# Moving the start addresses of the rounded weight halves in a two-block transformer kernel

## The chip, the cores and the metric

The kernel runs on one core of one Trainium2 chip. The metric is the device time of one execution in microseconds (us), from the first to the last instruction and what lies around it. Three runs of the kernel before gave 2228.66 us as the median, 2226.96 us the lowest and 2229.32 us the highest.

## The reference

Two transformer blocks run one after the other on 256 tokens of width 1024, all in float32, each with two layers. The first block has a modulated norm, a gated delta rule with 8 heads, a sliding-window attention with 16 heads, three projections and a gated feed-forward part with a short convolution. The second has a mixer (sparse attention chosen by an indexer, and a chunked mLSTM) between two feed-forward parts. Nearly all arithmetic is in products of the activations with large weight matrices:

```
for l in range(DEPTH):                       # first block
    proj = h @ w_in[l]                       # 1024 x 7440
    y_a = o_dn @ w_dn_out[l]; y_b = attention @ w_swa_out[l]
    x = x + gt1 * (merged @ w_o[l])
    up_act, up_lin = jnp.split(h @ w_up[l], 2, axis=-1)
    x = x + gt2 * ((jax.nn.silu(up_act) * up_lin) @ w_down[l])
for l in range(DEPTH):                       # second block
    x = x + 0.5 * swiglu(rmsnorm(x, ffn1_norm[l]), ffn1_w_gate[l], ffn1_w_up[l], ffn1_w_down[l])
    x = x + hybrid_mixer(...)                # h @ w_in, and @ w_out at its end
    x = x + 0.5 * swiglu(rmsnorm(x, ffn2_norm[l]), ffn2_w_gate[l], ffn2_w_up[l], ffn2_w_down[l])
```

## The kernel before

The weights stream through SBUF in chunks of 1 MB: eight blocks of 128 rows by 256 columns, or, for the products back from the hidden width, two blocks of 128 rows by 1024 columns. SP issues one DMA for a chunk into one of three ring slots (`ring`). To keep float32 precision with the faster rounded type of TensorE, a chunk is split into two halves. ScalarE copies it with rounding into the high half (`weights_high`, the `split` of the scalar block, line 2178); VectorE subtracts the high half from the ring slot and so makes the low half (`weights_low`, `split` of the vector block, line 1441). The activations are kept as a high and a low half too (`h_high`, `h_low`, and `hidden_high`, `hidden_low` in the feed-forward parts).

TensorE then makes three products for each tile of 128x128 weights: high weights by high activations, high weights by low activations, and low weights by high activations. In `linear3` these are lines 753, 754 and 755, in `linear3_tiles` 731 to 733 and in `down_tile` 991 to 993. Each of the three loads 128x128 weights as the stationary operand and streams 256 columns of activations, so a chunk is 48 pairs of a weight load and a matmul. `token_major3` (lines 784 to 786) has the roles exchanged: the activations are stationary and 256 columns of a weight half stream past.

Of the 314 chunks 304 are split. They are numbered n = 0 to 303 in the order of the schedule (`SPLIT`, `SI`). The halves of chunk n lie in pair n % 2 of two pairs of stores, so that one pair is written while the other is read. ScalarE waits, before it writes the high half of chunk n, until TensorE is done with chunk n - 2 (`chunk_multiplied`); VectorE waits for ScalarE (`chunk_rounded`), TensorE for VectorE (`chunk_split`). Two of the 304 chunks are wide ones with 272 columns a block (the first chunk of a layer of the first block, `s1`); the other 302 are called narrow here.

The four stores follow one another in the arena, 8768 bytes apart. In the built program they begin at bytes 127360, 136128, 144896 and 153664 of a partition. `shifts` lets each half begin 12 elements (48 bytes) into its store. The activation tiles (`h_high` at byte 52608, `h_low` at 60800, `hidden_high` at 70016) begin at 128 modulo 256. A row of a stationary tile is 512 bytes in a partition, and the tiles of a chunk lie multiples of 512 bytes apart, so that all tiles of one half have the same start modulo 256:

| half | store | start, bytes modulo 256 |
|---|---|---|
| high, even n | 0 | 176 |
| low, even n | 1 | 240 |
| high, odd n | 2 | 48 |
| low, odd n | 3 | 112 |

Of the kernel before, what the change touches and what calls it, by code (L numbers as in the profile page):

```python
# [20 lines left out]
T = 256  # L21
D = 1024
KT = D // P
# [8 lines left out]
WIDE = 272  # L32
# [142 lines left out]
def build(nc, a, out):  # L175
# [24 lines left out]
    with ExitStack() as ctx:  # L200
# [26 lines left out]
        def rounded(name, at, *shape):  # L227

            return nc.alloc_sbuf_tensor_at(name, [P] + list(shape), F32R, offset=arena_at + 4 * at)
# [12 lines left out]
        def ar(at, *shape):  # L242
            n = int(np.prod(shape))
            v = arena[:, at:at + n]
            if len(shape) == 2:
                return v.rearrange("p (a b) -> p a b", a=shape[0])
            if len(shape) == 3:
                return v.rearrange("p (a b c) -> p a b c", a=shape[0], b=shape[1])
            return v
# [18 lines left out]
        oH, oL = rounded("out_high", 8192, KT, T), rounded("out_low", 10240, KT, T)  # L268
        half_names = ("weights_high0", "weights_low0", "weights_high1", "weights_low1")
        half_stores = [rounded(n, 14336 + (SLOT + 16) * i, SLOT + 16) for i, n in enumerate(half_names)]  # L270
        shifts = (12, 12, 12, 12)
        half = lambda i, n: half_stores[i][:, shifts[i]:shifts[i] + KT * n].rearrange("p (t n) -> p t n", t=KT)
        WH, WL = ([half(2 * i + low, T) for i in range(2)] for low in range(2))
        wide_high, wide_low = ([half(2 * i + low, WIDE) for i in range(2)] for low in range(2))
        hW = ar(12288, KT, T)
        ktok = [ar(11264, 2, 2, P), ar(9216, 2, 2, P)]
        XV = ar(11264, 2, 512)
# [245 lines left out]
        def release(key):  # L523

            kind, l, i = key
            if kind == "turn":
                return rope_added, 5 * l + ROPE.index(i) + 1
            if kind == "adr":
                return mod_ready, GROUPS.index((l, i)) + 1
            if kind == "qkv":  # L530
                return conv_done, 12 * l + i + 1
            if kind == "qk":
                return (conv_scaled, 2 * l + i + 1) if i < 2 else (conv_done, 24 + 4 * l + i + 1)
            if kind in ("aq", "qi"):
                return q_scaled, 3 * l + 2 * (kind == "qi") + i + 1
            if kind in ("swq", "z", "ga", "gb", "vm", "om"):
                return in_copied, INC[key]
            if kind in ("dno", "swo"):
                return merged, 8 * l + 4 * (kind == "swo") + i + 1
            if kind == "wo":  # L540
                return x_done, X0["wo", l] + 2 * i + 2
            if kind == "out":
                return x_done, X0["out", l] + i + 1
            if kind == "ua":
                return fconv_done, FP * l + i + 1
            fi = {"ul": l, "g1": 2 + 2 * l, "u1": 2 + 2 * l, "g2": 3 + 2 * l, "u2": 3 + 2 * l}[kind]
            if kind[0] == "g":
                return gate_scaled, FP * (fi - 2) + i + 1
            return hidden_ready, FP * fi + i + 1
# [7 lines left out]
        for key in R:  # L557
            at = key[2] % 3 if key[0] == "qkv" else R[key] % 2
# [52 lines left out]
        def halves(n):  # L611

            if SPLIT[n][0] == "s1":
                return wide_high[n % 2][:, :, :], wide_low[n % 2][:, :, :]
            return WH[n % 2][:, :, :], WL[n % 2][:, :, :]

        landed = {}
        total = [0] * NS
# [94 lines left out]
        def _(pe):  # L713
# [3 lines left out]
            def linear3_tiles(key, high, low, order, pairs, made):  # L717

                n = SI[key]
                wh, wl = WH[n % 2], WL[n % 2]  # L720
                pe.wait_ge(chunk_split, n + 1)
                pe.wait_ge(*release(PREV[key]))
                o = PLACE[key]
                for m in range(2):
                    for t in order:
                        if pairs is not None and m == 0 and t < 4:
                            pe.wait_ge(pair_copied, pairs + t + 1)
                        if pairs is not None and m == 0 and t == 4:
                            pe.wait_ge(*made)
                        a_, b_ = wh[:, t, m * P:(m + 1) * P], wl[:, t, m * P:(m + 1) * P]  # L730
                        mm(o[:, m, :], a_, high[t], start=(t == order[0]), stop=False)
                        mm(o[:, m, :], a_, low[t], start=False, stop=False)
                        last = mm(o[:, m, :], b_, high[t], start=False, stop=(t == order[-1]))
                last.then_inc(chunk_multiplied, 1)

            def linear3(key, high, low, norm=None, ready=None, between=None):

                n = SI[key]
                wh, wl = WH[n % 2], WL[n % 2]
                pe.wait_ge(chunk_split, n + 1)  # L740
                if PREV[key] is not None:
                    pe.wait_ge(*release(PREV[key]))
                o = PLACE[key]
                for m in range(2):
                    for t in range(KT):
                        if (m, t) == (1, KT // 2) and between is not None:
                            between()
                        if norm is not None and m == 0:
                            pe.wait_ge(norm_ready, KT * norm + t + 1)
                        if ready is not None and m == 0 and t % 2 == 0:  # L750
                            pe.wait_ge(ready[0], ready[1] + t // 2 + 1)
                        a_, b_ = wh[:, t, m * P:(m + 1) * P], wl[:, t, m * P:(m + 1) * P]
                        mm(o[:, m, :], a_, high[:, t, :], start=(t == 0), stop=False)  # L753
                        mm(o[:, m, :], a_, low[:, t, :], start=False, stop=False)  # L754
                        last = mm(o[:, m, :], b_, high[:, t, :], start=False, stop=(t == KT - 1))  # L755
                last.then_inc(chunk_multiplied, 1)
# [15 lines left out]
            def token_major3(key, dst, norm=None):  # L772

                n = SI[key]
                wh, wl = halves(n)
                pe.wait_ge(chunk_split, n + 1)
                if key in R:
                    pe.wait_ge(*release(PREV[key]))
                for tt in range(2):
                    for t in range(KT):  # L780
                        if norm is not None and tt == 0:
                            pe.wait_ge(norm_ready, KT * norm + t + 1)
                        a_, b_ = h_high[:, t, tt * P:(tt + 1) * P], h_low[:, t, tt * P:(tt + 1) * P]
                        mm(dst(tt), a_, wh[:, t, :], start=(t == 0), stop=False)
                        mm(dst(tt), a_, wl[:, t, :], start=False, stop=False)
                        last = mm(dst(tt), b_, wh[:, t, :], start=False, stop=(t == KT - 1))
                last.then_inc(chunk_multiplied, 1)
# [191 lines left out]
            def down_start(kc, l, i, fi):  # L979

                n = SI[kc, l, i]
                pe.wait_ge(chunk_split, n + 1)
                pe.wait_ge(hidden_ready, FP * fi + i + 1)
                return (w[n % 2][:, :, :].rearrange("p a b -> p (a b)") for w in (WH, WL))

            def down_tile(wh, wl, i, t, m):

# [76 lines left out]
            def head_tiles(*tiles):  # L1064

                n = SI["s1", 0, 0]
                wh, wl = halves(n)
                pe.wait_ge(chunk_split, n + 1)
                for t in tiles:
                    pe.wait_ge(norm_ready, t + 1)  # L1070
                    for tt in range(2):
                        a_, b_ = h_high[:, t, tt * P:(tt + 1) * P], h_low[:, t, tt * P:(tt + 1) * P]
                        to = B[4 + tt][:, 0:WIDE]
                        mm(to, a_, wh[:, t, :], start=(t == 0), stop=False)
                        mm(to, a_, wl[:, t, :], start=False, stop=False)
                        last = mm(to, b_, wh[:, t, :], start=False, stop=(t == KT - 1))
                if tiles[-1] == KT - 1:
                    last.then_inc(chunk_multiplied, 1)
# [24 lines left out]
            for v in range(1, 8):  # L1103
                n = V_ROWS[v % 3] if v < 6 else V_ROWS[3]
# [204 lines left out]
            for l in range(LAYERS):  # L1309
# [79 lines left out]
                for c in range(2):  # L1389
                    for j in range(4):  # L1390
                        n = 4 * c + j
# [18 lines left out]
                for i in range(4):  # L1410
                    linear3_tiles(("out", l, i), merged_high, merged_low, range(KT), pairs if i == 0 else None, (m_split, l + 1))
# [1328 lines left out]
```

## Time and profile before

| | |
|---|---|
| median of three runs | 2228.66 us |
| the profiled execution | 2228.63 us |
| its span, first to last instruction | 2226.8 us |
| mean granted TensorE clock | 0.992 of full speed |
| TensorE matmuls (PE) busy | 2145.2 us, 96% of the span |
| TensorE weight loads (PEld) busy | 2043.7 us, 92% |
| VectorE (DVE) | 1505.3 us, 68% |
| ScalarE (ACT) | 1077.0 us, 48% |
| GpSimd (POOL) | 580.9 us, 26% |
| moved by DMA | 383.93 MB, 172 GB/s on average |

Matmuls are pipelined: the profile gives each a duration of some 280 ns, and the next one begins long before that has passed. How fast TensorE works is read from the distance of the starts. PE are the matmuls, PEld the weight loads; a wait is put down to the instruction that ended last before it was over.

### The profile page before, as it was taken

What the parts mean: (1) busy time and instruction counts of PE and PEld (TensorE: products, weight loads), DVE (VectorE), ACT (ScalarE), POOL (GpSimd) and SP (SyncE); (2) the same over time, 40 slices, a digit from 0 to 9 for tenths busy, and PEclk for the clock granted to TensorE, in tenths of its full rate; (3) what the DMA queues carried; (4) which work ended last, traced back from release to release, by engine and by line L of the source; (5) the groups of instructions that cost most, each with busy time, mean ns of one, the idle gap of its engine ahead of it and who ended that gap; (6) DMA issues with size and microseconds to landing.
All of it is one profiled execution on the core that took longest, in us unless ns stands there. A gap on an engine that the chain in (4) does not pass through costs nothing.

```text
span 2226.8 us, 39796 instructions
## 1 busy us (share of the span) xinstructions
PE 2145.2 (96%) x17221; PEld 2043.7 (92%) x17221; DVE 1505.3 (68%) x1850; ACT 1077.0 (48%) x1432; POOL 580.9 (26%) x280
## 2 busy tenths in 40 slices
PE   7999999999999999999999999989999999999999
PEld 4988899899998888989999999879999999879999
DVE  6967775787678766667666556876556556786555
ACT  3666573433356647443445435554445444555333
POOL 0963324899248260475000000100000000100000
PEclk9999999999999999999999999999999999999999
DMA  9752336677656315566555555335555555434553
GB/s 320 236 170 81 108 121 198 225 252 239 205 181 216 96 41 168 171 213 205 188 184 176 186 184 166 110 96 189 189 188 172 189 184 177 133 95 149 182 185 129
DMA packets 332856, 383.93 MB, mean 172 GB/s; under 512 B 12551, under 2 KB 315402, under 8 KB 332554
## 3 DMA queue, kind: packets, MB, share of 16 engines
q1 hardware_dynamic: 332234, 381.23, 53.6%
q8 instruction: 136, 2.23, 0.4%
q14 instruction: 38, 0.31, 0.0%
q10 hardware_dynamic: 448, 0.16, 0.0%
HBM read 380.32 MB, written 1.05 MB: 171 GB/s over the span
## 4 chain that ended last, share of the span: by engine, by line
PE 75%; DVE 15%; ACT 7%; issue 3%; DMA 0%; SPq 0%; ACTq 0%; DVEq 0%
PE bank L753 16%; PE bank L754 15%; PE bank L755 15%; DVE weights_low L1441 6%; PE bank L993 5%; PE bank L992 5%; PE bank L991 5%; ACT weights_high L2178 4%; DVE arena L1569 2%; PE bank L769 1%; PE bank L892 1%; PE bank L1210 1%; PE bank L1225 1%; PE bank L884 1%; PE bank L1047 1%
## 5 line engine op out<-in xcount | busy, mean ns | idle before, releaser
L1441 DVE TENSOR_TENSOR weights_low<-ring,weights_high 128x2048 fp32r<-128x2048 f32 (+1 forms) x304 | 759.2, 2497 | 431.6 <-ACT weights_high L2178 431.0
L753 PE MATMUL bank<-h_high,weights_high 128*128 128x256 f32 x3296 | 937.9, 285 | 23.7 <-DVE weights_low L1441 14.3
L755 PE MATMUL bank<-h_high,weights_low 128*128 128x256 f32 x3296 | 925.8, 281 | 0.0
L754 PE MATMUL bank<-h_low,weights_high 128*128 128x256 f32 x3296 | 923.0, 280 | 0.0
L2178 ACT ACTIVATE weights_high<-ring 128x2048 fp32r<-128x2048 f32 (+1 forms) x304 | 582.2, 1915 | 693.3 <-PE bank L755 537.1
L753 PEld LDWEIGHTS bank<-h_high,weights_high 128*128 128x128 f32 x3296 | 622.0, 189 | 43.4 <-DVE weights_low L1441 23.8
L754 PEld LDWEIGHTS bank<-h_low,weights_high 128*128 128x128 f32 x3296 | 620.6, 188 | 3.4 <-issue 3.3
L755 PEld LDWEIGHTS bank<-h_high,weights_low 128*128 128x128 f32 x3296 | 620.3, 188 | 0.0
L991 PE MATMUL bank<-hidden_high,weights_high 128*128 128x256 f32 x1056 | 295.3, 280 | 1.4 <-DVE hidden_low L1707 0.9
L993 PE MATMUL bank<-hidden_high,weights_low 128*128 128x256 f32 x1056 | 296.2, 281 | 0.0
L992 PE MATMUL bank<-hidden_low,weights_high 128*128 128x256 f32 x1056 | 295.2, 280 | 0.0
L2657 POOL TENSOR_TENSOR side<-side,ccol 128x1024 f32<-128x1024 f32 x80 | 206.2, 2598 | 305.4 <-DVE out_low L1674 133.0
L2635 POOL TENSOR_TENSOR side<-swq 128x512 f32<-128x512 f32 x4 | 8.2, 2076 | 814.0 <-DVE swq L2022 814.0
L991 PEld LDWEIGHTS bank<-hidden_high,weights_high 128*128 128x128 f32 x1056 | 199.1, 189 | 2.0 <-issue 1.1
L992 PEld LDWEIGHTS bank<-hidden_low,weights_high 128*128 128x128 f32 x1056 | 198.3, 188 | 0.0
L993 PEld LDWEIGHTS bank<-hidden_high,weights_low 128*128 128x128 f32 x1056 | 198.3, 188 | 0.0
L2658 POOL TENSOR_TENSOR side<-side 128x1024 f32<-128x1024 f32 x40 | 127.3, 3181 | 3.1
L1569 DVE SCALAR_TENSOR_TENSOR arena<-bank,vcol,arena 128x254 f32<-128x254 f32 (+2 forms) x256 | 111.3, 476 | 3.7
L2659 POOL TENSOR_TENSOR side<-side 128x512 f32<-128x512 f32 x40 | 85.1, 2129 | 3.1
L2329 ACT ACTIVATE hidden_high<-arena 128x512 fp32r<-128x512 f32 x66 | 41.0, 621 | 72.0 <-DVE arena L1704 72.0
L1717 DVE TENSOR_TENSOR arena<-bank,rinv 128x512 f32<-128x512 f32 x44 | 30.4, 692 | 56.3 <-PE bank L755 50.5
L1704 DVE TENSOR_TENSOR arena<-arena,bank 128x512 f32<-128x512 f32 x66 | 45.1, 684 | 33.6 <-DVE arena L1720 27.7
(439 smaller groups left out, 2817.7 us busy)
## 6 DMA issues: line engine op xcount, KB each, us to landing
ring<-in_w_in SPq DMA_DIRECT2D x80, 1024.0 KB, 5.3
ring<-in_w_up SPq DMA_DIRECT2D x44, 1024.0 KB, 5.3
ring<-in_ffn_w_gate SPq DMA_DIRECT2D x44, 1024.0 KB, 5.4
ring<-in_ffn_w_up SPq DMA_DIRECT2D x44, 1024.0 KB, 5.4
ring<-in_ffn_w_down SPq DMA_DIRECT2D x44, 1024.0 KB, 5.0
side<-in_w_ada SPq DMA_DIRECT2D x42, 1024.0 KB, 7.8
ring<-in_w_down SPq DMA_DIRECT2D x22, 1024.0 KB, 5.0
ring<-in_w_dn_out SPq DMA_DIRECT2D x8, 1024.0 KB, 5.2
```

The costliest lines, as they stand in the source:

```text
L753: mm(o[:, m, :], a_, high[:, t, :], start=(t == 0), stop=False)
L754: mm(o[:, m, :], a_, low[:, t, :], start=False, stop=False)
L755: last = mm(o[:, m, :], b_, high[:, t, :], start=False, stop=(t == KT - 1))
L991: mm(o, wh[:, cols], high, start=(i == 0 and t == 0 and m % 2 == 0), stop=False, skip_group_check=True)
L992: mm(o, wh[:, cols], low, start=False, stop=False, skip_group_check=True)
L993: return mm(o, wl[:, cols], high, start=False, stop=(i == FP - 1 and t == 1), skip_group_check=True)
L1441: v.tensor_tensor(low, wide(q), high.bitcast(F32), ALU.subtract).then_inc(chunk_split, 1)
L1569: ins = [v.scalar_tensor_tensor(out=dst[:, m, s:T], in0=ps[:, m, 0:T - s], scalar=cols(taps - 1 - s, m), in1=dst[:, m, s:T], op0=ALU.mult, ...
L2178: a_(halves(n)[0], wide(q), ACT.Copy).then_inc(chunk_rounded, 1)
L2657: then(*[g_.tensor_tensor(w[:, u:u + 4, :], w[:, u:u + 4, :], bcast(ccol[:, u:u + 4], 256), ALU.mult) for u in (0, 4)])
L2658: then(g_.tensor_tensor(w[:, 0:4, :], w[:, 0:4, :], w[:, 4:8, :], ALU.add))
L2659: then(g_.tensor_tensor(w[:, 0:2, :], w[:, 0:2, :], w[:, 2:4, :], ALU.add))
```

## The change

Only addresses change. `narrow(n)` takes the place of the fixed views `WH` and `WL`, in `halves` (which the two `split` functions and `token_major3` use), `linear3`, `linear3_tiles` and `down_start`:

```diff
-        shifts = (12, 12, 12, 12)
-        half = lambda i, n: half_stores[i][:, shifts[i]:shifts[i] + KT * n].rearrange("p (t n) -> p t n", t=KT)
-        WH, WL = ([half(2 * i + low, T) for i in range(2)] for low in range(2))
-        wide_high, wide_low = ([half(2 * i + low, WIDE) for i in range(2)] for low in range(2))
+        PLACE_OF, PLACES = (24, 56), 32
+        half = lambda i, at, n: half_stores[i][:, at:at + KT * n].rearrange("p (t n) -> p t n", t=KT)
+        wide_high, wide_low = ([half(2 * i + low, 12, WIDE) for i in range(2)] for low in range(2))
+
+        def narrow(n):
+
+            i, place = n % 2, n // 6 % PLACES
+            return half(2 * i, PLACE_OF[i] + 2 * (place // 16), T), half(2 * i + 1, PLACE_OF[i] + 4 * (place % 16), T)
...
             if SPLIT[n][0] == "s1":
                 return wide_high[n % 2][:, :, :], wide_low[n % 2][:, :, :]
-            return WH[n % 2][:, :, :], WL[n % 2][:, :, :]
+            return narrow(n)
...
             def linear3(key, high, low, norm=None, ready=None, between=None):
 
                 n = SI[key]
-                wh, wl = WH[n % 2], WL[n % 2]
+                wh, wl = narrow(n)
```

The offsets are counted in elements of 4 bytes. Both high halves now begin at 224 bytes modulo 256. The place of chunk n is n // 6 modulo 32. In places 16 to 31 (n from 96 to 191, and the start of a second pass at n from 288 on) the high halves begin 8 bytes further on, at 232. The low halves begin at 32 bytes modulo 256 in places 0 and 16, and 16 bytes further on with each place, through all sixteen multiples of 16. Both pairs of stores have the same start modulo 256 at a given place. The wide chunks stay where they were. The instructions of every engine, their number, their order and their waits are the same.

## Rows read from the trace of the kernel before

**Rows 1.** The page: busy time and share of each engine.
```profile
span 2226.8 us, 39796 instructions
PE 2145.2 (96%) x17221; PEld 2043.7 (92%) x17221; DVE 1505.3 (68%) x1850; ACT 1077.0 (48%) x1432; POOL 580.9 (26%) x280
```
**Rows 2.** The page: the chain of work that ended last, by engine and line.
```profile
PE 75%; DVE 15%; ACT 7%; issue 3%; DMA 0%; SPq 0%; ACTq 0%; DVEq 0%
PE bank L753 16%; PE bank L754 15%; PE bank L755 15%; DVE weights_low L1441 6%; PE bank L993 5%; PE bank L992 5%; PE bank L991 5%; ACT weights_high L2178 4%; DVE arena L1569 2%; PE bank L769 1%; PE bank L892 1%; PE bank L1210 1%; PE bank L1225 1%; PE bank L884 1%; PE bank L1047 1%
```
**Rows 3.** Who waited for whom, PE: waited for, us in total, times, longest.
```profile
PE bank L753 <- DVE weights_low L1441: 16.1, 31, 1.5
```
**Rows 4.** Timeline, PE: start us, us, what; chunks 197 and 225 begin.
```profile
1531.79 0.28 PE L991 MATMUL bank<-hidden_high,weights_high 128*128 128x256 f32 x1
...
1689.71 0.28 PE L991 MATMUL bank<-hidden_high,weights_high 128*128 128x256 f32 x1
```
**Rows 5.** That stretch: us, busy us (x count) of each engine, PEclk, DMA share.
```profile
1531.79:1689.71 157.92, 157.92 (x1346) 157.92 (x1345) 88.73 (x66) 63.55 (x47) 0.00 (x0) 1.00 0.58 187
```
**Rows 6.** Timeline, PE: the first matmuls of chunks 209 to 213.
```profile
1599.47 0.28 PE L991 MATMUL bank<-hidden_high,weights_high 128*128 128x256 f32 x1
...
1605.10 0.28 PE L753 MATMUL bank<-h_high,weights_high 128*128 128x256 f32 x1
...
1610.75 0.28 PE L753 MATMUL bank<-h_high,weights_high 128*128 128x256 f32 x1
1610.87 0.28 PE L754 MATMUL bank<-h_low,weights_high 128*128 128x256 f32 x1
1610.99 0.28 PE L755 MATMUL bank<-h_high,weights_low 128*128 128x256 f32 x1
...
1616.38 0.28 PE L991 MATMUL bank<-hidden_high,weights_high 128*128 128x256 f32 x1
...
1622.03 0.28 PE L753 MATMUL bank<-h_high,weights_high 128*128 128x256 f32 x1
```
**Rows 7.** Groups of instructions in the stretch of rows 5: count, busy, mean ns.
```profile
L753 PEld LDWEIGHTS bank<-h_high,weights_high 128*128 128x128 f32 x288 | 54.3, 189 | 0.0
L1441 DVE TENSOR_TENSOR weights_low<-ring,weights_high 128x2048 fp32r<-128x2048 f32 x28 | 64.2, 2293 | 48.7 <-ACT weights_high L2178 48.7
L2178 ACT ACTIVATE weights_high<-ring 128x2048 fp32r<-128x2048 f32 x28 | 53.7, 1919 | 94.7 <-PE bank L755 65.8 <-PE bank L993 28.8
```
**Rows 8.** Timeline, PE: 16 pairs from tiles at 128 modulo 256, 128 columns.
```profile
1080.09 1.95 PE L1028 MATMUL bank<-constants,acc 128*128 128x128 f32 x16
1081.79 0.36 PE L753 MATMUL bank<-h_high,weights_high 128*128 128x256 f32 x1
```
**Rows 9.** Timeline, PE: first and last matmul of chunk 186, with exchanged roles.
```profile
1403.20 0.28 PE L784 MATMUL bank<-weights_high,h_high 128*128 128x256 f32 x1
...
1408.74 0.28 PE L786 MATMUL bank<-weights_high,h_low 128*128 128x256 f32 x1
```

More of the change, by code:

```diff
@@ L738, in linear3 @@
                 n = SI[key]
-                wh, wl = WH[n % 2], WL[n % 2]
+                wh, wl = narrow(n)
                 pe.wait_ge(chunk_split, n + 1)
@@ L983, in down_start @@
                 pe.wait_ge(hidden_ready, FP * fi + i + 1)
-                return (w[n % 2][:, :, :].rearrange("p a b -> p (a b)") for w in (WH, WL))
+                return (w.rearrange("p a b -> p (a b)") for w in narrow(n))
             def down_tile(wh, wl, i, t, m):
```

## The prediction

> **What bounds the kernel now.** I began with the busy shares of the page [rows 1]: matmuls are under way for 96% of the span, VectorE for 68%, ScalarE for 48%. The chain that ended last [rows 2] says the same by line: TensorE has 75% of it, and the six lines of the three-product scheme alone have 61%. VectorE's low halves and ScalarE's high halves have 6% and 4% of it, in the parts where they are late, and the list of waits gives the largest such wait of a matmul as 16.1 us in total [rows 3]. So most of the time is the pace at which TensorE takes pairs of a weight load and a matmul, and this pace is what an address could alter.
>
> A matmul's duration of 0.28 us does not show the pace; the starts do. From the first matmul of chunk 197 to that of chunk 225 pass 157.92 us [rows 4], without an idle moment on PE or on the weight loads, at the full granted clock, the level of 2.4 GHz [rows 5]. That is 28 chunks, 5.640 us each, and with 48 pairs a chunk 117.5 ns a pair. The 302 narrow chunks are 14496 pairs, and at 117.5 ns they are 1703 us of the span of 2226.8 us. The other 524 us are other matmuls, the two wide chunks and waits.
>
> The trace of before holds a small experiment on the very thing that is changed, since even and odd chunks have different addresses. I took the starts of chunks 209 to 213 [rows 6]: the odd ones, 209 and 211, last 5.63 us each (1599.47 to 1605.10, 1610.75 to 1616.38), the even ones, 210 and 212, 5.65 us (1605.10 to 1610.75, 1616.38 to 1622.03). Chunk 209 is a product of another kind than 210 to 212, so kind does not decide it; 210 and 211 are of one kind and differ. So the address does reach the pace: high at 48 and low at 112 modulo 256 is quicker by 0.02 us a chunk, 0.4 ns a pair, than high at 176 and low at 240.
>
> **The change part by part.** No instruction is added, removed or moved, on any engine or queue; SP's transfers go into the ring slots, which stay. What can differ is the duration of three things.
>
> *ScalarE and VectorE write the halves at other starts.* They take 1.919 and 2.293 us [rows 7], one after the other 4.21 us of a chunk's 5.64. In the 157.92 us of 28 chunks ScalarE stood idle for 94.7 us before its copies, waiting for TensorE to free the store, and that is their cover. I cost this part at nothing. Were the cover gone, as in the parts in which TensorE waits for a low half, a write slower by a tenth would add 0.4 us for each of the 31 waits [rows 3], 12 us. Every write of before, at four starts, is within the same means, so I do not expect it.
>
> *TensorE loads the high half from 224, later 232.* Two of three pairs load it, 9664 of the 14496. *It loads the low half from sixteen starts in turn*, in 4832 pairs. The trace has no row at these starts, so both are bounded by near rows. The nearest are the two pairs of starts of before. If all chunks went like the odd ones, the 150 or so even chunks would each save 0.02 us: 3 us less. If all went like the even ones, 3 us more. The far lower bound is a stretch in which stationary and moving tiles both begin at 128 modulo 256: 16 pairs, each with 128 columns, begin within 1.70 us [rows 8], 106 ns a pair. This is 11.5 ns under 117.5, and on the high pairs alone 9664 x 11.5 ns = 111 us. But these stream half the columns in another number format, so it is a far row. The upper bound is a pace of 120 ns, the distance that the timeline prints as 0.12 between the three matmuls that open chunk 211 [rows 6]: 2.5 ns on all pairs, 36 us.
>
> Between ends so far apart I go by the nearest row, and that gives no sign: the four starts of before have a spread of 0.4 ns, and I see no way to order 224, 232 and the sixteen low starts by it. A second row speaks for a pace that hardly hangs on the start of a half. In chunk 186 the activations, at 128 modulo 256, are loaded, and the weight halves stream [rows 9]. From its first to its last matmul, 47 distances, pass 5.54 us, 117.9 ns. Start and role of the weights are exchanged there, and the pace is within 0.4 ns. I take zero for both terms. The sum is the profiled execution's 2228.63 us plus nothing, rounded to 2228 us; this execution is within 0.03 us of the median of the three runs, so no correction is needed.
>
> The Trainium skill, in "TensorE: Matmul & The Clock Gate", section Back-to-back issue gap, gives N / 2.4 + 2.5 ns for a lone stream of matmuls, whatever the addresses, an estimate of 109.2 ns for 256 columns. The trace disagrees on the size, 117.5 ns, and rows 6 disagree on the indifference to addresses, by 0.4 ns. By that formula the sum would be zero as well.
>
> **The rivals.**
>
> *Slower by the 8 bytes.* A weight row of 512 bytes that begins at a multiple of 16 is 32 pieces of 16 bytes. From 232 modulo 256 it begins and ends in half a piece and so is 33. This holds for the high halves of places 16 to 31, 112 chunks (n from 96 to 191 and from 288 to 303), with 32 high loads each, 3584 loads. If reading pieces sets the pace, each costs 1/32 of 117.5 ns, 3.7 ns: 13 us, and 2241 us in all. It decides (over 0.2%, 4.5 us, about what a measurement of this kernel can tell from no change) from 1.3 ns a load on. Against it: a load is only half of a pair, and a load of 189 ns [rows 7] overlaps its neighbours; no row of before begins off a multiple of 16. It would show as a step in the pace at n = 96. The Trainium skill, "SBUF — State Buffer", table of specifications, has 16-byte cachelines in SBUF and a penalty for each crossing into another. No run so far shows it.
>
> *Slower by the turning low halves.* The low starts visit all phases, and both halves leave the start of 48 modulo 64 that all four had. If three quarters of the low pairs, 3624, ran at 120 ns, this would be 9 us more, 2237 us. For it speaks only that starts matter at all [rows 6].
>
> *Faster by the high start.* Both pairs of stores now have one and the same high start. If 224 suits the stream of activations better than 48 does by as much as three or four times the spread seen, 1.5 ns, the 9664 high pairs give 14 us: 2214 us. Rows 8 show that a pair can go far quicker. The cover of the splits is enough for this, since a chunk would last 5.59 us.
>
> *The change does nothing*, because the true cause of rows 6 is the parity of the store and not the start modulo 256: this lies within my forecast.
>
> **How the numbers follow.** I give the forecast, a pace within the band of the two pairs of stores and a little around it, 43%; the time is 2228 us, and it reaches from 2222 to 2234. Of the 43, 33 are within 0.2%, 5 on each side beyond. Faster by the high start has 30%, slower by the 8 bytes 15%, slower by the low halves 12%. So faster has 0.35, the same 0.33, slower 0.32. The range has to reach both groups of rivals: from 2208 us, some way past 2214, to 2246 us, past 2241. It leaves out about one in ten on each side, where a pace nearer to rows 8 or to 120 ns would lie.
>
> **What would show it.** The number of matmuls and the clock must be the same. Right: chunks without a wait last 5.62 to 5.66 us throughout, whatever the place. The starts of chunks 197 and 225 are 157.92 us apart, give or take 0.5. Rival of the 8 bytes: chunks 96 to 191 are slower by up to 0.12 us each than those just before and after. Low halves: the length of a chunk rises and falls with the place, within every 96 chunks. High start: all chunks shorter by 0.05 us or more. Wrong altogether: if ScalarE's copies or VectorE's subtractions change from 1.92 and 2.29 us, or if TensorE's waits for `weights_low` grow by more than some microseconds, since I gave these nothing.

## The result and the profile after

The changed kernel takes 2235.43 us (median of 5 runs, 2234.88 to 2236.59), the kernel before 2226.96 us beside it (5 runs, 2223.82 to 2229.32). The ratio is 1.0037 with a 95% interval of 1.0025 to 1.0049: slower by 8.5 us, clear of noise. The profiled execution took 2235.43 us too.

The changed page has the same instructions as [rows 1], and TensorE is again the engine under way for 96% of a longer span:

```profile
span 2233.6 us, 39796 instructions
PE 2150.8 (96%) x17221; PEld 2050.4 (92%) x17221; DVE 1503.1 (67%) x1850; ACT 1078.2 (48%) x1432; POOL 581.4 (26%) x280
```

Lines have moved by five: 753 of before is 758 now, 991 is 996, 1441 is 1446, 2178 is 2183. The timeline of the changed kernel on PE, the first matmuls of chunks 197 and 225, answers to [rows 4]. Behind them stands what the window view says of this stretch, as in [rows 5]:

```profile
1536.92 0.28 PE L996 MATMUL bank<-hidden_high,weights_high 128*128 128x256 f32 x1
...
1696.21 0.28 PE L996 MATMUL bank<-hidden_high,weights_high 128*128 128x256 f32 x1
```
```profile
1536.92:1696.21 159.29, 159.29 (x1346) 159.29 (x1345) 88.70 (x66) 63.65 (x47) 0.00 (x0) 1.00 0.57 185
```

The same 28 chunks take 159.29 us where they took 157.92, with the same count of matmuls, no idle moment and the full granted clock in both. So the time was lost inside the stream of pairs. The groups of the stretch, against [rows 7]:

```profile
L1446 DVE TENSOR_TENSOR weights_low<-ring,weights_high 128x2048 fp32r<-128x2048 f32 x28 | 64.2, 2292 | 49.2 <-ACT weights_high L2183 49.2
L758 PEld LDWEIGHTS bank<-h_high,weights_high 128*128 128x128 f32 x288 | 54.1, 188 | 0.0
L2183 ACT ACTIVATE weights_high<-ring 128x2048 fp32r<-128x2048 f32 x28 | 53.8, 1921 | 95.9 <-PE bank L760 66.7 <-PE bank L998 29.3
```

The writes take 2292 and 1921 ns (2293 and 1919 before), a weight load 188 (189). None of the durations shows the loss; only the starts do. TensorE's largest wait for a low half did not grow either; it was 16.1 us [rows 3] and is

```profile
PE bank L758 <- DVE weights_low L1446: 14.4, 28, 1.5
```

Within the stretch the pace changes with the place of a chunk. The timeline of the changed kernel on PE, the first matmuls of chunks 198, 204, 210 and 216, where places 1 to 4 begin:

```profile
1542.60 0.28 PE L758 MATMUL bank<-h_high,weights_high 128*128 128x256 f32 x1
...
1576.85 0.28 PE L758 MATMUL bank<-h_high,weights_high 128*128 128x256 f32 x1
...
1610.77 0.28 PE L758 MATMUL bank<-h_high,weights_high 128*128 128x256 f32 x1
...
1645.31 0.28 PE L758 MATMUL bank<-h_high,weights_high 128*128 128x256 f32 x1
```

Six chunks last 34.25, 33.92 and 34.54 us, which is 118.9, 117.8 and 119.9 ns a pair (over 288 pairs). The high half begins at 224 in all three; only the low half's start moved, 48, 64, 80.

Collisions of TensorE's reads with the writes of the other engines would be another cause. I sorted the distances between starts in the 28 chunks by what else was under way. While VectorE wrote a low half the mean was 118.51 ns, while ScalarE wrote a high half 118.52, and while neither did 118.53 (before: 117.47, 117.50 and 117.53). The loss is the same with and without a write, so these writes are not its cause.

For the comparisons below I took a pace for every chunk: the mean distance between the starts of its 48 matmuls, without distances over 140 ns, which are waits, other matmuls between, or stretches at the lower granted clock. Over chunks 1 to 303 it is 117.51 ns before and 118.34 ns in the changed kernel. The difference of 0.83 ns makes 12 us on 14496 pairs, but the span grew by 6.8 us. The waits do not hold the rest: those that the waits view lists for PE sum to 76.8 us before and 77.9 after. The granted clock does. The mean over the span was 0.992 before and 0.994 after:

```profile
core 0: 2233.6 us, clock 0.994
```

The clock fell to 1.2 GHz for 37.5 us of the profiled execution before and for 28.6 us of the one after, in a few short stretches. One of them lay in chunk 267 of before. The window view of that stretch, and below it that of the same chunk in the changed kernel:

```profile
2009.30:2012.70 3.40, 3.40 (x18) 3.40 (x18) 2.07 (x1) 0.00 (x0) 0.00 (x0) 0.51 0.06 8
2016.20:2019.60 3.40, 3.40 (x31) 3.40 (x31) 2.06 (x1) 0.00 (x0) 0.00 (x0) 1.00 0.12 15
```

At half the clock 18 matmuls are under way in 3.40 us, at the full clock 31. If each microsecond at the lower clock loses half a microsecond, 8.9 us less of it give back 4.5 us, and 12 less 4.5 is 7.5 us, near the 6.8 us measured. This is an estimate; no run shows why one execution was granted more of the full clock than another.

### The profile page after: what moved, and what is told of

Its sections match the earlier page's. It is cut to its first block, busy times and chain, and to the rows that moved or that the text cites. A ratio compares the mean times of both kernels' runs of the same rounds, so it can differ in the third digit from the quotient of the medians.

```text
span 2233.6 us, 39796 instructions
## 1 busy us (share of the span) xinstructions
PE 2150.8 (96%) x17221; PEld 2050.4 (92%) x17221; DVE 1503.1 (67%) x1850; ACT 1078.2 (48%) x1432; POOL 581.4 (26%) x280
## 4 chain that ended last, share of the span: by engine, by line
PE 75%; DVE 14%; ACT 7%; issue 3%; SPq 1%; DMA 0%; ACTq 0%; DVEq 0%
PE bank L758 16%; PE bank L759 16%; PE bank L760 16%; DVE weights_low L1446 6%; PE bank L998 5%; PE bank L997 5%; PE bank L996 5%; ACT weights_high L2183 3%; DVE arena L1574 2%; PE bank L774 1%; PE bank L897 1%; PE bank L1215 1%; PE bank L1230 1%; PE bank L889 1%; PE bank L1033 1%
```

## The experiments

Twelve kernels ran. Eleven differ from the changed kernel only in how the starts are chosen; one differs from the kernel before. Their results in one table, with "pace" as defined above, "28 chunks" the time from the start of chunk 197 to that of chunk 225, and "low clock" the time at 1.2 GHz. The last four columns are of the one profiled execution:

| run | high, low start modulo 256 | median us | ratio to before (95%) | 28 chunks, us | mean pace, ns | span, us | low clock, us |
|---|---|---|---|---|---|---|---|
| before | 176, 240 even; 48, 112 odd | | 1 | 157.92 | 117.51 | 2226.8 | 37.5 |
| change | 224 or 232, turning | 2235.43 | 1.0037 (1.0025 to 1.0049) | 159.29 | 118.34 | 2233.6 | 28.6 |
| e1 | 48, 112 | 2221.61 | 0.9966 (0.9953 to 0.9979) | 157.44 | 117.25 | 2222.3 | 36.2 |
| e2 | 176, 240 | 2227.60 | 0.9998 (0.9989 to 1.0008) | 158.30 | 117.80 | 2224.5 | 24.3 |
| e3 | 176 or 48, turning | 2233.86 | 1.0021 (1.0012 to 1.0031) | 158.66 | 118.19 | 2234.1 | 37.5 |
| e4 | 224 or 232, 240 or 112 | 2233.16 | 1.0020 (1.0011 to 1.0030) | 159.13 | 118.16 | 2233.1 | 34.5 |
| e5 | 224, turning | 2233.41 | 1.0025 (1.0015 to 1.0034) | 159.29 | 118.21 | 2230.4 | 24.7 |
| e6 | turning, high + 64 | 2230.51 | 1.0012 (1.0002 to 1.0021) | 159.06 | 118.06 | 2231.0 | 34.1 |
| e7 | 224, 240 | 2234.38 | 1.0032 (1.0022 to 1.0042) | 158.78 | 118.17 | 2233.5 | 34.7 |
| e8 | turning, 112 | 2232.43 | 1.0021 (1.0011 to 1.0030) | 158.84 | 118.05 | 2229.5 | 25.1 |
| e9 | 112, 176 | 2217.22 | 0.9935 (0.9912 to 0.9959) | 155.30 | 116.60 | 2215.9 | 37.5 |
| e10 | 112, turning | 2230.31 | 1.0009 (0.9999 to 1.0018) | 158.77 | 117.94 | 2227.8 | 27.3 |
| e11 | as before, everything 64 bytes on | 2230.08 | 1.0000 (0.9991 to 1.0010) | 157.92 | 117.53 | 2230.5 | 41.0 |
| e12 | 112, 224 | 2215.49 | 0.9939 (0.9926 to 0.9953) | 156.80 | 116.78 | 2215.1 | 35.7 |

The kernel before, run again beside them, had medians of 2228.06 to 2229.19 us. Reckoned from the span of before by the pace alone (14496 pairs times the difference), the spans come out up to 6.7 us off. With half a microsecond added or taken for each microsecond more or less at the low clock, all are within 3 us. So a difference of a few microseconds between two kernels is read from the pace first, and from the time only at the same clock.

**e1 and e2: fixed starts, the same in both pairs of stores.**

```diff
-        PLACE_OF, PLACES = (24, 56), 32
+        PLACE_OF, PLACES = (44, 12), 32        # e1;  (12, 44) in e2
...
-            return half(2 * i, PLACE_OF[i] + 2 * (place // 16), T), half(2 * i + 1, PLACE_OF[i] + 4 * (place % 16), T)
+            return half(2 * i, PLACE_OF[i], T), half(2 * i + 1, PLACE_OF[i], T)
```

> Both pairs of stores get the starts that the odd chunks had before: high at 48, low at 112 modulo 256. Theory A (the start modulo 256 sets the pace of a chunk, which store it is does not): even chunks go at the odd pace of before, 5.62 to 5.63 us instead of 5.65 to 5.66, so 151 narrow even chunks x 0.03 us, 4.5 us less than before; the distance from the start of chunk 197 to that of chunk 225 falls from 157.92 to about 157.5 us. Theory B (the parity of the store sets it): even chunks stay at 5.65 us, time as before. Theory C (only the turning itself costs, any fixed starts are alike): time as before, and chunks alike.

> Both pairs of stores get the starts that the even chunks had before: high at 176, low at 240 modulo 256. Theory A (starts set the pace): odd chunks go at 5.65 to 5.66 us too, 4.5 us more than before, about half of what the whole change cost; chunks 197 to 225 take 158.3 us. Theory B (the store sets it): odd chunks stay at 5.62 to 5.63 us, time as before.

The timeline of e1 on PE, first matmuls of chunks 209, 210 and 211, and then that of e2:

```profile
1598.62 0.28 PE L996 MATMUL bank<-hidden_high,weights_high 128*128 128x256 f32 x1
...
1604.25 0.28 PE L758 MATMUL bank<-h_high,weights_high 128*128 128x256 f32 x1
...
1609.87 0.28 PE L758 MATMUL bank<-h_high,weights_high 128*128 128x256 f32 x1
```
```profile
1599.73 0.28 PE L996 MATMUL bank<-hidden_high,weights_high 128*128 128x256 f32 x1
...
1605.39 0.28 PE L758 MATMUL bank<-h_high,weights_high 128*128 128x256 f32 x1
...
1611.04 0.28 PE L758 MATMUL bank<-h_high,weights_high 128*128 128x256 f32 x1
```

In e1 the even chunk 210 takes 5.62 us (5.65 before), in e2 the odd chunk 209 takes 5.66 us (5.63 before). The store is not the cause; the start is. Theory B falls, and so does theory C, since two fixed pairs of starts differ. The median of e1 is 7 us lower, where 4.5 were expected. Its profiled execution, 2224.10 us, is 4.5 us below that of before at the same mean clock, 0.992; the other four took 2220.29 to 2221.62 us, and no trace shows why. In e2 the pace rose as expected, from 117.51 to 117.80 ns, or 4 us on all pairs, but the time did not: the ratio's interval takes in no change. The clock hides it. All ten runs of e2 had a mean clock of 0.993 to 0.995, and 22 of the 26 runs of before beside them had 0.990 to 0.992. At 0.995 the six of e2 have a median of 2227.3 us, the two of before took 2223.4 and 2224.3.

**e3 and e4: one half of the change at a time.**

```diff
+            return half(2 * i, 12, T), half(2 * i + 1, PLACE_OF[i] + 4 * (place % 16), T)         # e3
+            return half(2 * i, PLACE_OF[i] + 2 * (place // 16), T), half(2 * i + 1, 12, T)         # e4
```

> The low halves turn as in the change, the high halves stay at 176 (even) and 48 (odd). If the low starts cost the time (rival of the turning low halves): most of the 8.5 us stays, 6 to 9 us above before, and single places are slow. If the high start costs it: within 2 us of before. If it is the pair of both starts that counts: slow places, but other ones than in the changed kernel, and even and odd chunks of one place differ.

> The high halves begin at 224 (232 in places 16 to 31) as in the change, the low halves stay at 240 (even) and 112 (odd). If the high start costs the time: 6 to 9 us above before. If the 8 bytes cost it: chunks 96 to 191 slower than the rest by up to 0.12 us. If the low starts cost it: within 2 us of before. If the pair counts: even chunks go like the changed kernel's places with the low half at 240 (13 and 29) and odd ones like those with it at 112 (5 and 21), 118.2 and 117.8 ns a pair.

Against the before beside them, e3 and e4 are 5.1 and 4.4 us slower by the medians, and the change was 8.5 us slower than its own. That looks like two halves of a whole, but the pace says otherwise: 0.68 ns for the low part alone, 0.65 for the high part alone, 0.83 for both. Either one costs most of what both cost, 9.9 and 9.4 us on all pairs against 12, and they do not add up. In single chunks the pair of starts counts. The median pace of the chunks with the same low start, ns:

| low start | high 48 (e3, odd) | high 112 (e10) | high 176 (e3, even) | high 224 (e5) |
|---|---|---|---|---|
| 80 | 117.4 | 119.8 | 118.2 | 119.5 |
| 112 | 117.4 | 120.0 | 117.8 | 117.8 |
| 176 | 118.5 | 115.6 | 117.8 | 117.8 |

No row and no column is slow or quick throughout. Of e4's forecasts by pairs the even chunks came out (118.15 ns with 224 and 240, as place 13 had), the odd ones did so only in part: of 96 chunks with 224 and 112, 40 went at 117.7 to 118.0 ns, as the change's place 5 had, and 56 at 118.3 to 118.7. So the pair of starts does not say all. Nor does the 119.5 of the table: with 224 and 80 e5 went near 118.0 ns in 8 of the 12 chunks of its first two passes, and at 119.6 to 120.0 in all six of the third.

**e5: without the 8 bytes.**

```diff
+            return half(2 * i, PLACE_OF[i], T), half(2 * i + 1, PLACE_OF[i] + 4 * (place % 16), T)
```

> The change without its 8 bytes: the high halves begin at 224 modulo 256 in every place, the low halves turn as in the change. Rival of the 8 bytes: chunks 96 to 191 get faster, up to 13 us less than the changed kernel. Theory A (what counts is which pair of starts a chunk has, and 232 is just another start): the time stays within 2 us of the changed kernel's 2235.4, since its places 16 to 31 had 118.36 ns a pair on average and places 0 to 15 had 118.28; but single places change, place 25 from 119.6 to place 9's 117.7 ns, place 17 from 118.2 to place 1's 118.9.

It is 2.0 us below the changed kernel, and the intervals of the two ratios overlap. Within the change, the mean pace of chunks 96 to 191 was 118.36 ns against 118.28 in the narrow ones of chunks 1 to 95 and 192 to 287. In the same chunks 96 to 191 e5 had 117.99 ns, 0.36 less, which is 1.7 us; the rival's 3.7 ns a load would have been 2.5 ns a pair. Some 0.15 of the 0.36 ns come from one place, where e5 (high 224, low 240) went at 115.5 ns in this pass and at 118.2 and 118.1 in the two others. Single places did change as expected. The timelines of the change and of e5 on PE, first matmuls of chunks 150 and 156, between which lies place 25 (low half at 176):

```profile
1189.85 0.28 PE L758 MATMUL bank<-h_high,weights_high 128*128 128x256 f32 x1
...
1224.57 0.28 PE L758 MATMUL bank<-h_high,weights_high 128*128 128x256 f32 x1
```
```profile
1190.17 0.28 PE L758 MATMUL bank<-h_high,weights_high 128*128 128x256 f32 x1
...
1224.36 0.28 PE L758 MATMUL bank<-h_high,weights_high 128*128 128x256 f32 x1
```

With the high half at 232 the six chunks take 34.72 us, at 224 34.19 us. Elsewhere it is the other way round: place 23 had 117.7 ns a pair at 232 and 118.9 at 224. A start 8 bytes on acts as another start; a cost of its own is far below the rival's, and a few tenths of a nanosecond are not excluded. The Trainium skill ("SBUF — State Buffer", section Specifications (TRN2)) states a penalty for each crossing into another 16-byte cacheline. Here a row of 512 bytes has one crossing more, and a penalty of the size priced does not show.

**e6, e7 and e8: both halves turning, a fixed pair, the high half turning.** The kernels e6 to e10 and e12 are made by

```diff
+        STORE_AT = (128, 192, 0, 64)
...
+            return tuple(half(j, (start - STORE_AT[j]) % 256 // 4, T) for j, start in ((2 * i, high_start(n)), (2 * i + 1, low_start(n))))
```

with `high_start` and `low_start` of 16 * (n // 6 % 16) and 64 more in e6, 224 and 240 in e7, 16 * (n // 6 % 16) and 112 in e8.

> High halves begin at 16 bytes times the place modulo 256, low halves 64 bytes behind them, in both pairs of stores, with a new place every six chunks, 16 places. Before, the change's place 0, and both earlier fixed pairs had this distance of 64. If the distance of the two halves sets the pace: all places alike. If the start against the activations sets it too: places differ, place 3 (48 and 112) at 117.2 ns, place 11 (176 and 240) at 117.7, place 14 (224 and 32) at 117.9 to 118.4. If a start at a multiple of 64 is what is slow: places 0, 4, 8 and 12 stand out.

> All narrow chunks have their high half at 224 and their low half at 240 modulo 256. In the run with the high part alone 93 of its 151 even chunks had these starts; most went at 118.15 ns a pair, but 5 at 115.5. If the starts alone set the pace: 118.15 ns throughout, 9 us more than before. If the pace also depends on the moment at which a chunk is entered, and a chunk hands it on to the next of the same starts: long runs of chunks at 115.5 ns, up to 28 us less than before.

> The low halves stay at 112 modulo 256 in both pairs of stores, the high halves begin at 16 bytes times the place. If the pair of starts sets the pace, place 3 (48 and 112) goes at 117.2 ns, place 14 (224 and 112) at 117.7 to 118.7, and the sixteen places spread from 117 to 120 as they do when the low halves turn; the average near 118.3, 10 us more than before. If the high start matters less than the low one, the spread is smaller.

In e6 the distance of the halves stays at 64 and the median paces of the places still run from 115.6 to 119.9 ns; multiples of 64 do not stand out (115.8, 117.8, 117.8 and 118.3 ns at 0, 64, 128 and 192). The quickest place is 7, starts 112 and 176. In e8 the high start spreads the places as much as the low one did in the change, from 117.1 (at 160) to 120.0 (at 0 and 16), so it matters as much. e7 did not become quick: 118.0 to 118.5 ns in nearly all chunks, and chunks at 115.5 to 116.2 ns only in one place, two in a row.

**e9: the quickest pair of e6, everywhere.** `high_start` is 112, `low_start` 176.

> All narrow chunks have their high half at 112 and their low half at 176 modulo 256, place 7 of the run in which both halves turned. There these starts went at 115.6 ns a pair in the second and third pass, and at 117.8 in the first. If a chunk hands its rhythm on to the next of the same starts and the quick one is steady: up to 1.9 ns x 14496 pairs = 27 us less than before, 2200 us. If the quick rhythm is lost at every wait: 117.8 ns in most chunks, 4 us more than before. Theory of the starts alone (no rhythm): all chunks alike.

This is faster than both kernels, 2217.22 us, with runs from 2206.29 to 2217.94. The lowest had a mean clock of 0.996, the three others 0.992; by the estimate above that is some 10 of the 11 us between them. The trace, of a run at 0.992, shows two rhythms. The window view of e9, for the stretch from chunk 197 to 225 and for that from chunk 231 to 258:

```profile
1524.03:1679.33 155.30, 155.30 (x1346) 155.30 (x1345) 88.72 (x66) 63.49 (x47) 0.00 (x0) 1.00 0.59 190
1717.08:1869.72 152.64, 152.64 (x1299) 152.64 (x1297) 85.11 (x63) 61.07 (x45) 0.00 (x0) 1.00 0.59 187
```

155.30 us for 28 chunks is 115.6 ns a pair, 152.64 us for 27 chunks is 117.8. Instructions, starts, clock and other engines' work are alike. Of 303 chunks 171 went at under 116.3 ns and 124 between 117.4 and 118.2. Between them lie waits. The timeline of e9 on PE, first matmul of chunk 226:

```profile
1685.64 0.36 PE L760 MATMUL bank<-h_high,weights_high 128*128 128x256 f32 x1 [0.60 <-DVE h_low L1532]
```

I counted all neighbours. In 155 pairs of chunks without a start distance over 140 ns the rhythm never changed; in the 147 pairs with one it changed 51 times, with the line between the rhythms at 117 ns. Of the 147, 81 held waits and nothing else, with 27 changes; the others also held other matmuls or a stretch at the lower clock. The stream keeps its rhythm as long as it is unbroken, and may come out of a break with the other.

**e10: high at 112, the low half turning.**

> High halves at 112 modulo 256 everywhere, low halves begin at 16 bytes times the place. If it is the high start that makes the quick rhythm, many places go near 115.6 ns and the whole is 10 us or more quicker than before. If it is the pair, only place 11 (low at 176) is quick, place 7 (low at 112) near the 117.3 that 112 and 112 had when the high half turned alone, the others spread from 117.7 to 120, and the whole is 5 to 10 us slower than before.

The pair, not the high start, makes the pace: with 112 the places go from 115.6 (low at 176) to 120.0 ns (low at 112), and the whole is as fast as before. The forecast for place 7 failed in most chunks: 112 and 112 had a median of 117.4 ns in e8 and 120.0 here. Both are rhythms of this pair, since 4 of the 18 chunks here went at 117.4 and one of the 18 in e8 at 120.0. Place 14 (low at 224) was near 116.7 ns in all three passes, with no second rhythm.

**e11: everything 64 bytes on.** From the kernel before:

```diff
+        apart = sb("apart", P, 16)
         h_high = sb("h_high", P, KT, T, dt=F32R)
```

> The kernel before with 64 unused bytes ahead of the activation halves, so that activations and weight halves all begin 64 bytes further on, and their distances stay. If only the distances between the tiles that are read together set the pace: even and odd chunks as before, 117.7 and 117.1 ns, the time within 2 us of before. If the weights' own start sets it: even chunks (240 and 48) and odd ones (112 and 176) go as these pairs do elsewhere, the odd ones at 115.6 or 117.8 ns.

The timeline of e11 on PE, first matmuls of chunks 209 to 213, against [rows 6]:

```profile
1602.99 0.28 PE L992 MATMUL bank<-hidden_high,weights_high 128*128 128x256 f32 x1
...
1608.61 0.28 PE L754 MATMUL bank<-h_high,weights_high 128*128 128x256 f32 x1
...
1614.27 0.28 PE L754 MATMUL bank<-h_high,weights_high 128*128 128x256 f32 x1
...
1619.89 0.28 PE L992 MATMUL bank<-hidden_high,weights_high 128*128 128x256 f32 x1
...
1625.55 0.28 PE L754 MATMUL bank<-h_high,weights_high 128*128 128x256 f32 x1
```

Chunks of 5.62 and 5.66 us by turns: the difference of even and odd chunks of before, with all four halves at other absolute starts (even 240 and 48, odd 112 and 176). The ratio is 1.0000. The absolute starts of the weight halves alone do not set the pace: odd chunks had those of e9 here and went at 117.1 ns, without its 115.6, and even chunks those of e6's place 15, which went at 117.8 to 120.1. What stayed the same is the distance between the tiles that are read one beside the other, the weight halves and the activations. Only this one shift was tried, and it leaves every start modulo 64 as it was, so that the distances alone set the pace is shown for 64 bytes and no further.

**e12: a pair with one rhythm.** `high_start` is 112, `low_start` 224.

> All narrow chunks have their high half at 112 and their low half at 224 modulo 256. In the run with the high half at 112 and the low one turning, these starts (places 14, 30 and 46) went near 116.7 ns a pair in every pass. If this pair has only one rhythm: all chunks near 116.7 ns, 0.8 ns x 14496 pairs = 12 us less than before, about 2216 us, and a smaller spread between runs than with 112 and 176, whose runs went from 2206 to 2218. If it has a second rhythm too, long runs of chunks at another pace, and a time between 2206 and 2235.

The timeline of e12 on PE, first matmuls of chunks 197 and 225, then 231 and 258:

```profile
1527.39 0.28 PE L998 MATMUL bank<-hidden_high,weights_high 128*128 128x256 f32 x1
...
1684.19 0.28 PE L998 MATMUL bank<-hidden_high,weights_high 128*128 128x256 f32 x1
...
1721.81 0.28 PE L760 MATMUL bank<-h_high,weights_high 128*128 128x256 f32 x1
...
1873.01 0.28 PE L998 MATMUL bank<-hidden_high,weights_high 128*128 128x256 f32 x1
```

156.80 us for 28 chunks and 151.20 us for 27 are both 116.7 ns a pair. Of 303 chunks 292 lie within 0.3 ns of it; six of the others have the exchanged roles and went at 117.6 to 117.8. The median is 2215.49 us, the runs lie between 2215.18 and 2216.88, and the forecast was 2216. It is the best of the fixed versions by its median: 13.7 us below the kernel before that ran beside it, 20 below the changed one.

## Why the prediction was wrong

The forecast was no change, 2228 us, and the kernel is 8.5 us slower. The range of 2208 to 2246 us held the time by its width, and slower had 0.32.

- The stretch of 28 chunks was to take 157.92 us, give or take 0.5, and took 159.29. Its chunks of 5.65 to 5.76 us left the 5.62 to 5.66 that were named as the sign of being right.
- *What bounds the kernel* was right: TensorE's stream of pairs at 117.5 ns, and the address reaches it. Rows 6 were a real effect of the starts (e1, e2), and the writes by ScalarE and VectorE cost nothing, as put.
- *The step that failed* is the pricing of the two weight terms by their nearest row: "I go by the nearest row, and that gives no sign", zero for both. The spread of 0.4 ns between two pairs of starts was taken for the size of the effect. Over many pairs the paces run from 115.5 to 120.0 ns, and most lie at 117.7 and above. The two pairs of before, at 117.7 and 117.1, are in the quicker half of what the sweeps found. To leave them for other starts costs 0.65 to 0.83 ns a pair in e3, e4, e5 and the change alike. Put at zero, the low term measured 9.9 us by the pace and 5.1 by the medians, the high term 9.4 and 4.4, each alone; the two together 12 us by the pace and 8.5 by the medians. The medians are smaller in part because most runs of e3 and e4 had a higher mean clock (0.993 and 0.994) than those of before beside them. That the two terms could be priced apart and added was a second flaw: the pace goes with the pair of starts, and the two costs do not add.
- *The second row for a small effect*, chunk 186 at 117.9 ns, was one more sample, and I read it as a sign that starts hardly matter. It was a chance value: the same chunk went at 115.5 ns in e9 and at 120.1 in e6, so starts matter with exchanged roles too.
- *The rival of the turning low halves* was nearest, at 2237 us: its sign, and its mark that chunk lengths rise and fall with the place, came true. Its price of 9 us for the low part alone is near the 9.9 us by the pace in e3. That the whole came out near 2237 us is in part luck: the high start alone costs as much (e4), the two do not add, and the price was a pace of 120 ns in three quarters of the low pairs, which no trace shows.
- *The rival of the 8 bytes* fell at its price (e5). The step of 2.5 ns at chunk 96 is not there; at most 0.36 ns is.
- *Faster by the high start* was wrong for 224, and a high start by itself is not a cause: at 112 with the low half turning nothing is gained (e10). With a fitting low half e9 and e12 gain 12 to 14 us. That this is the 14 us priced is chance, as the 1.5 ns behind it had no row.
- The upper bound of 120 ns was the slowest rhythm found. The lower one, 106 ns, was never approached; the quickest rhythm was 115.5 ns.

Open is what in the reading of the tiles makes one distance slower than another, why the same pair of starts can hold two rhythms, and which of the two a break leaves behind. No run here shows a unit that would explain it. The sorting by what the other engines write was even before and in the change, but not in e12 (116.3, 117.2 and 116.7 ns). Each pace comes from one trace of its kernel, and no second one shows whether another run of it takes the same rhythms. Starts other than multiples of 16 bytes were tried only with the high half at 232.

## What to carry to other kernels

Where TensorE's stream is unbroken for hundreds of microseconds, read the pace from the starts of matmuls, many chunks apart, since the printed durations do not show it. If two buffers of a double-buffered operand go at different paces, their places relative to the other operand are worth a sweep: turn the start chunk by chunk inside one kernel, read the pace of each place from one trace, and then fix the quickest that has only one rhythm. A sweep is a measurement; it costs what the average start costs. Before a few microseconds between two kernels are explained, compare the mean granted clock of their runs: a stretch at the lower clock can lose up to half its length.

## What was not expected of the hardware

The pace of pairs of a 128x128 weight load and a 256-column matmul holds steady values between 115.5 and 120.1 ns, to a tenth over many chunks, at the full granted clock; 115.6, 116.7, 117.1, 117.7, 118.9 and 120.0 came up most. It changes with the starts of the weight halves and did not change when all tiles moved by 64 bytes (e11), and it does so while the load still prints 187 to 190 ns and the other engines' writes take as long as before. Some pairs of starts have two rhythms, 115.6 and 117.8 ns in e9, 117.4 and 120.0 with 112 and 112, and only a break took the stream from one to the other (51 changes in e9's 147 neighbours with a break, none in 155 without).

The time at the lower clock differed between kernels with the same instructions, from 24.3 to 41.0 us in the profiled executions, which by the estimate above is worth up to 7 us against the kernel before. No run shows why it differed.
